# Hybrid attention layer, 16 heads in pairs: scores with q's high and low parts stacked in 128 rows

## What is computed

```python
h = rms_norm(x, norm_pre_g)
proj = einsum('bsd,de->bse', h, w_in)          # q, k, v, gate for 2 groups of 8 heads x 64, and 8 forget columns
# group A, per head:  logit[t,s] = q_t.k_s/8 + F[t] - F[s], causal, softmax, times v   (F: cumulated log forget gate)
# group B, per head:  logit[t,s] = q_t.k_s/8 - slope * (t - s), causal, softmax, times v
y = concat(y_a * silu(g_a), y_b * silu(g_b))
out = x + rms_norm(y @ w_out, norm_post_g)
```

## Time and profile before

| | before |
|---|---|
| median of 3 runs | 153.03 us |
| lowest, highest | 152.94, 153.65 us |
| profiled execution | 154.46 us |
| its span | 152.5 us |
| granted TensorE clock, mean | 0.977 of full speed |
| PE, DVE, ACT, POOL busy | 93%, 74%, 63%, 32% of the span |

### The profile page before, as it was taken

How to read it: one execution, slowest core, us unless ns; L and a number is a source line. 1 busy time by engine, 2 the same in 40 slices (tenths; PEclk the granted TensorE clock), 3 DMA queues, 4 the chain that set the end, 5 groups by cost and what they waited for, 6 DMA issues and landing times.

```text
span 152.5 us, 2938 instructions
## 1 busy us (share of the span) xinstructions
PE 142.0 (93%) x1020; PEld 133.6 (88%) x1020; DVE 112.8 (74%) x241; ACT 96.8 (63%) x199; POOL 48.1 (32%) x67
## 2 busy tenths in 40 slices
PE   7993999999999999999899999999999999999940
PEld 7992899999999989998899999999999888898840
DVE  0644918799999898856979897998979797220493
ACT  5455786717991799489487778686776855215430
POOL 7500000000000000708329393919375574201230
PEclk9999599999999999999999999999999999999995
DMA  3889995497789779880846463636451180000034
GB/s 106 233 255 390 392 373 181 148 349 254 241 258 315 260 299 413 314 267 9 221 156 192 140 198 132 210 140 209 138 171 35 49 295 0 0 4 0 0 116 160
DMA packets 14524, 29.05 MB, mean 191 GB/s; under 512 B 2472, under 2 KB 7088, under 8 KB 14128
## 3 DMA queue, kind: packets, MB, share of 16 engines
q1 hardware_dynamic: 14064, 27.57, 53.7%
q10 hardware_dynamic: 448, 1.32, 2.2%
HBM read 25.73 MB, written 1.06 MB: 176 GB/s over the span
## 4 chain that ended last, share of the span: by engine, by line
PE 64%; DVE 20%; DMA 5%; ACT 4%; SPq 3%; issue 1%; DVEq 0%; ACTq 0%
PE bank L801 26%; PE bank L960 15%; DVE w_lo L549 9%; PE bank L811 9%; PE bank L913 6%; DMA raw<-in_w_f 5%; ACT w_hi L369 3%; DVE wo_lo L630 2%; DVE h L594 2%; PE bank L894 2%; PE bank L896 2%; PE bank L895 2%; SPq L202 2%; DVE gate L638 2%; DVE v L607 1%
## 5 line engine op out<-in xcount | busy, mean ns | idle before, releaser
L549 DVE TENSOR_TENSOR w_lo<-raw,w_hi 128x1024 fp32r<-128x1024 f32 (+1 forms) x34 | 47.1, 1386 | 8.0 <-ACT w_hi L369 7.6
L369 ACT ACTIVATE w_hi<-raw 128x1024 fp32r<-128x1024 f32 (+1 forms) x34 | 35.8, 1059 | 6.2 <-DVE logits L645 3.6
L801 PE MATMUL bank<-h_hi,w_hi 128*128 128x256 f32 x128 | 35.8, 280 | 0.4 <-DVE h_lo L650 0.4
L801 PE MATMUL bank<-h_lo,w_hi 128*128 128x256 f32 x128 | 35.7, 279 | 0.0
L801 PE MATMUL bank<-h_hi,w_lo 128*128 128x256 f32 x128 | 35.7, 279 | 0.0
L306 POOL TENSOR_TENSOR bias<-squares,causal 128x256 f32<-128x256 f32 (+1 forms) x8 | 12.0, 1525 | 55.0 <-DMA squares<-decay_rows_scratch 55.0
L801 PEld LDWEIGHTS bank<-h_hi,w_hi 128*128 128x128 f32 x128 | 24.1, 188 | 1.1 <-DVE h_lo L650 0.6
L801 PEld LDWEIGHTS bank<-h_lo,w_hi 128*128 128x128 f32 x128 | 24.0, 188 | 0.5
L801 PEld LDWEIGHTS bank<-h_hi,w_lo 128*128 128x128 f32 x128 | 24.0, 188 | 0.0
L323 POOL TENSOR_TENSOR probs<-probs,row_inv 128x256 f32<-128x256 f32 (+1 forms) x16 | 12.9, 828 | 29.4 <-DVE row_inv L681 29.4
L464 ACT ACTIVATE probs<-logits,neg_max 128x128 f32<-128x128 f32 (+1 forms) x32 | 14.2, 445 | 7.8 <-DVE neg_max L675 7.8
(11 more groups left out here) (118 smaller groups left out, 308.7 us busy)
## 6 DMA issues: line engine op xcount, KB each, us to landing
raw<-in_w_units SPq DMA_DIRECT2D x30, 512.0 KB, 4.1
raw_out<-in_w_out SPq DMA_DIRECT2D x4, 512.0 KB, 4.6
v_pair<-v SPq DMA_DIRECT2D x8, 256.0 KB, 3.9
raw<-in_w_out SPq DMA_DIRECT2D x4, 512.0 KB, 3.4
h<-in_x SPq DMA_DIRECT2D x1, 1024.0 KB, 9.0
squares<-decay_rows_scratch ACTq DMA_DIRECT2D x1, 1024.0 KB, 8.0
x_t<-in_x SPq DMA_DIRECT2D x1, 1024.0 KB, 5.0
raw<-in_w_units SPq DMA_DIRECT2D x3, 256.0 KB, 4.3
```

The lines of the kernel that those rows point to most:

```text
L369: nc.scalar.activation(w[0][:, s, 0:width], raw[:, s, 0:width], ACT.Copy).then_inc(s_hi, 1)
L549: nc.vector.tensor_tensor(w[1][:, s, 0:width], raw[:, s, 0:width], w[0][:, s, 0:width].bitcast(F32), ALU.subtract).then_inc(s_lo, 1)
L801: last = nc.tensor.matmul(dst, stationary(a, j), moving(b, j), start=n == 1, stop=n == count * len(PASSES))
```

## The change

- q_hi becomes q_both (128 x 2 buffers x 2 heads x 256). For head a, ACT writes the high part in the head's own 64 rows (two instructions of 64 rows instead of one of 128). The other 64 rows get the head's q_lo by DMA.
- q_lo is made by two DVE instructions of 64 rows.
- k_wide_hi becomes k_twice: own rows k high from ACT, the other 64 rows the same k high, copied by DMA in place of zeros. k_lo keeps its zeros.
- The scores: per head, q_both x k_twice (high x high and low x high in one product over 128 rows) and q_both x k_lo (high x low). Eight matmuls of one head's 128 or 256 columns in place of six of 256 or 512.
- SP issues four copies per pair, 64 rows of 1 KB each: q_across(i), two, after q_lo(i); k_across(i), two, after k_hi(i). For pair 0 they stand ahead of SP's loop, for pair i in the loop's turn i: q_across between the two loads, k_across behind them.
- PE's scores wait for both pairs of copies and for k_lo.
- probs is the same buffer as logits; the row of ones moves to y32; one memset of POOL goes.

```diff
-        q_hi = sb("q_hi", [P, 2, SEQ], F32R)
+        q_both = sb("q_both", [P, 2, 2, SEQ], F32R)
-        k_wide = [sb(f"k_wide_{n}", [P, 2, SEQ], F32R) for n in PARTS]
+        k_twice, k_lo = sb("k_twice", [P, 2, SEQ], F32R), sb("k_lo", [P, 2, SEQ], F32R)
-        probs = sb("probs", [P, 2, NB])
+        probs = logits
...
+            def q_across(i):
+                sp.wait_ge(s_qlo, i + 1)
+                for a in range(2):
+                    sp.dma_start(q_both[head_rows[1 - a], i % 2, a, :].bitcast(F32),
+                                 q_lo[head_rows[a], i % 2, :].bitcast(F32)).then_inc(s_q_across[i % 2], 16)
+
+            def k_across(i):
+                sp.wait_ge(s_khi, 2 * i + 2)
+                for a in range(2):
+                    sp.dma_start(k_twice[head_rows[1 - a], a, :].bitcast(F32),
+                                 k_twice[head_rows[a], a, :].bitcast(F32)).then_inc(s_k_across[i % 2], 16)
+
+            q_across(0)
+            k_across(0)
             for i in range(1, PAIRS + 1):
...
-                for u in range(QK_0 + 6 + 2 * i, QK_0 + 8 + 2 * i):
+                for n, u in enumerate(range(QK_0 + 6 + 2 * i, QK_0 + 8 + 2 * i)):
+                    if i < PAIRS and n == 1:
+                        q_across(i)
                     if u < UNITS:
                         load_unit(u // RING, u % RING)
...
+                if i < PAIRS:
+                    k_across(i)
...
             def query_high(i, b):
...
-                nc.scalar.activation(q_hi[:, b, :], bank[0][:, 0:SEQ], ACT.Copy).then_inc(s_qhi, 1)
+                for a, own in enumerate(head_rows):
+                    nc.scalar.activation(q_both[own, b, a, :], bank[0][own, 0:SEQ], ACT.Copy).then_inc(s_qhi, 1)
...
             def query_low(i, b):
-                dve.wait_ge(s_qhi, i + 1)
-                nc.vector.tensor_tensor(q_lo[:, b, :], bank[0][:, 0:SEQ], q_hi[:, b, :].bitcast(F32),
-                                        ALU.subtract).then_inc(s_qlo, 1)
+                dve.wait_ge(s_qhi, 2 * i + 2)
+                for a, own in enumerate(head_rows):
+                    ins = nc.vector.tensor_tensor(q_lo[own, b, :], bank[0][own, 0:SEQ], q_both[own, b, a, :].bitcast(F32),
+                                                  ALU.subtract)
+                ins.then_inc(s_qlo, 1)
...
-            def scores(i, b):
-                pe.wait_ge(s_qhi, i + 1)
-                pe.wait_ge(s_qlo, i + 1)
-                pe.wait_ge(s_khi, 2 * i + 2)
+            def scores(i, b, loads):
+                pe.wait_ge(s_q_across[b], 32 * loads)
+                pe.wait_ge(s_k_across[b], 32 * loads)
                 pe.wait_ge(s_klo, 2 * i + 2)
                 for dst, rows, keys in ((s0_ps, slice(0, P), P), (s1_ps, slice(P, SEQ), SEQ)):
-                    nc.tensor.matmul(dst, q_hi[:, b, rows], k_wide[0][:, :, 0:keys], start=True, stop=False)
-                    nc.tensor.matmul(dst, q_hi[:, b, rows], k_wide[1][:, :, 0:keys], start=False, stop=False)
-                    last = nc.tensor.matmul(dst, q_lo[:, b, rows], k_wide[0][:, :, 0:keys], start=False, stop=True)
+                    for a in range(2):
+                        nc.tensor.matmul(dst[:, a, :], q_both[:, b, a, rows], k_twice[:, a, 0:keys],
+                                         start=a == 0, stop=False)
+                        last = nc.tensor.matmul(dst[:, a, :], q_both[:, b, a, rows], k_lo[:, a, 0:keys],
+                                                start=False, stop=a == 1)
                 last.then_inc(s_qk, 1)
```

More of the change, by code:

```diff
@@ L53 @@
 WARM_UP = 12
-N_CONST = 4
+N_CONST = 3
 PASSES = ((0, 0), (0, 1), (1, 0))
@@ L119, in hybrid_layer @@
         decay_row = logits[0:HEADS, 0, 0:SEQ]
-        ones_row = probs[0:HEADS, 0, 0:SEQ]
+        probs = logits
+        ones_row = y32[0:HEADS, :]
         junk = squares[:, :, :].rearrange("p a b -> p (a b)").rearrange("p (t d) -> p t d", t=TT)
@@ L171, in hybrid_layer @@
         s_khi, s_klo = sem("k_hi"), sem("k_lo")
+        s_q_across = [sem(f"q_lo_across{b}") for b in range(2)]
+        s_k_across = [sem(f"k_hi_across{b}") for b in range(2)]
         s_qk = sem("scores_ready")
@@ L282, in _ @@
                                base=0, pattern=[[-1, P]], channel_multiplier=1).then_inc(s_const, 1)
-            for part in k_wide:
-                pool.memset(part[:, :, :].bitcast(F32), 0.0).then_inc(s_const, 1)
+            pool.memset(k_lo[:, :, :].bitcast(F32), 0.0).then_inc(s_const, 1)
             pool.memset(ones_row, 1.0).then_inc(s_const, 1)
@@ L479, in key_high @@
                 for a, own in enumerate(head_rows):
-                    nc.scalar.activation(k_wide[0][own, a, :], bank[1][own, 0:SEQ], ACT.Copy).then_inc(s_khi, 1)
+                    nc.scalar.activation(k_twice[own, a, :], bank[1][own, 0:SEQ], ACT.Copy).then_inc(s_khi, 1)
             def gates_silu():
@@ L690, in key_low @@
                 for a, own in enumerate(head_rows):
-                    nc.vector.tensor_tensor(k_wide[1][own, a, :], bank[1][own, 0:SEQ],
-                                            k_wide[0][own, a, :].bitcast(F32), ALU.subtract).then_inc(s_klo, 1)
+                    nc.vector.tensor_tensor(k_lo[own, a, :], bank[1][own, 0:SEQ],
+                                            k_twice[own, a, :].bitcast(F32), ALU.subtract).then_inc(s_klo, 1)
             def gated(i):
@@ L931, in _ @@
             query(1, 1)
-            scores(0, 0)
+            scores(0, 0, 1)
             key(1, 1)
@@ L941, in attend @@
                 pe.wait_ge(s_logits, 4 * i - 4)
-                scores(i - 1, 1 - b)
+                scores(i - 1, 1 - b, loads + b)
                 key(i, b)
@@ L970, in _ @@
             pe.wait_ge(s_logits, 4 * PAIRS - 4)
-            scores(PAIRS - 1, 1)
+            scores(PAIRS - 1, 1, PAIRS // 2)
             out_part(1, range(0, 2))
```

## The result

The changed kernel takes 166.1 us in the median (165.59 to 167.66) against 152.99 for the kernel before on the same chip: a ratio of 1.084, with an interval of 1.0794 to 1.0885, or 13 us more. It is slower, as forecast, but by more than twice the 6 us and outside the range (162.5).

The account below looks back on a forecast made before the run. PE was taken as the bound, with a period of 8.33 us per pair and DVE's loop as long in the second half. Delay at scores(1) 5.6 plus 0.4 over pairs 2 to 7 gave +6.0: 159.0 us, range 156.0 to 162.5.

Parts of the forecast that it names:

- PE's new products: Scores on PE: 128-column matmuls taken at 0.11 us, 256-column ones at 0.12; a group 0.91 us, 0.15 less than now.
- the rival of plain f32 speed: Scores on PE: 128-column products cost 0.23 us each, group 1.39 us, total 160.8 us; chance 0.27.
- my 1.2: Scores on PE over eight pairs: 1.2 us saved by columns alone, if nothing waits.
- Pair 0, copies: Before scores(0): PE waits 2.6 us for the second key copy, issued at 64.6 and landed at 67.6.
- Pair 1: Before scores(1): key copy held behind SP's load waiting for unit_low, lands at 78.55; scores 5.6 us later, the main term.
- The clock: Rival: PE's clock falls behind the waits before scores(0) and scores(1), 0 to 1.6 us more, 160.6; chance 0.12.
- DVE's split: Two q_lo instructions of 64 rows: +0.43 us per pair on DVE, its loop 8.82 us, setting pairs 5 to 7.
- pairs 2 to 7: Six periods at 0.15 less give back 0.9 us, waits cost about 1.3: net +0.4 us.
- The faster rival: Copies land before their scores everywhere, 151.8 us; tested by pair 1's copy landing before k_lo(1) is done; chance 0.04.

Follow-up runs that it names:

- experiment 4: Changed kernel without the copies (their rows zeros) and without DVE's two q_lo instructions: ratio 0.9896 to the kernel before, -1.6 us.
- experiment 2: Changed kernel with the key's copy of pair 1 issued ahead of SP's load that waits for unit_low: ratio 1.0525 to the kernel before, +8.0 us.
- experiment 1: Changed kernel with idle PE products ahead of scores(0) and around transposes(0) to fill the waits: ratio 1.0653 to the kernel before, +10.0 us.
- experiment 8: Kernel of experiment 2 with 24 idle products ahead of scores(0): ratio 1.0529 to the kernel before, +8.1 us.
- experiment 7: Changed kernel without the copies, with four same-size transfers at their places into a buffer nobody reads: ratio 1.0147 to the kernel before, +2.2 us.
- experiment 5: Kernel before with only q_hi and q_lo each split into two instructions of 64 rows: ratio 1.0209 to the kernel before, +3.2 us.

## Why the prediction was wrong, point by point

**PE's new products: right.** The 128-column matmuls stand 0.11 us apart:

```profile
127.36 0.27 PE L918 MATMUL bank<-k_lo,q_both 128*128 128x128 f32 x1
127.47 0.27 PE L916 MATMUL bank<-k_twice,q_both 128*128 128x128 f32 x1
127.58 0.28 PE L918 MATMUL bank<-k_lo,q_both 128*128 128x128 f32 x1
```

Those with 256 columns stand 0.12 apart (128.03 to 128.38 in the chain above). So the rival of plain f32 speed (0.23) is out. The 81 ns that the Trainium skill (TensorE: Matmul & The Clock Gate, Back-to-back issue gap) gives is not reached here: the measured 0.11 decides. The group at 127.20, behind a wait, takes 1.18 us to 128.38, against 1.29 for the one at 72.94. Without hindrance the change gives 1.6 us (0.6 to 2.6, experiment 4), against my 1.2, though not all of that is PE's.

**Pair 0, copies: right, 1.0 us too small.** Scores(0) were to start 2.6 us late and started at 67.15, 2.3 later in the trace (64.83 before, in PE's timeline) and 3.6 counted from query(0). By the trace the copy of q_lo released it, which landed in 3.4 us; I had named the key's. Waits, place and order were as forecast.

**Pair 1: right mechanism, term mis-sized.** The delay was to grow by 3.0 us and grew by 5.2. Three items make it: the second copy lands in 3.5 us where I took 2.6; an issue takes 0.55 where I took 0.35, twice; and scores(0) ran at the lower clock (2.07 us from 67.15 to their end at 69.22 instead of 1.1). That SP's load ahead of the copy makes the wait long is shown by experiment 2.

**The clock: the step that failed.** I gave it 0.12 and at most 1.6 us, arguing that the work behind the waits has slack. It has none: the scores and the key product behind the second wait are the path, and they took 0.75 and 2.0 us more than at the full clock. The second fall cost 2.9 us (experiment 1), on top of 1 us within pair 1. I also took three microseconds at 0.50 from the earlier trace rows, and here the lower clock lasted over 6 us, twice. Without these 3.9 us the kernel would have taken some 162 us (my estimate, 166.1 less the two terms), just inside the range.

The trace before had the evidence that a fall was to be expected. The idle stretches of PE in all ten traces of this case bear it out, and show where it stops: behind each of the six of 2.3 us and more (2.34, 2.41, 2.64, 3.18, 3.21, 3.24) the granted clock went to the lower level. Of those between 1.6 and 2.1 us it did so behind three (1.64 in experiment 8, 2.04 in experiment 1, 2.08 in experiment 7) and not behind four (1.68, 1.77, 2.00, 2.08). Behind the shorter ones it never did. So a wait of 2.6 or 4 us should have carried the fall in the forecast and not in a rival.

**DVE's split: under-priced, and the engine that makes PE wait misnamed.** I took 0.43 us per pair from the durations of 64-row instructions. The right number is from start to start, 0.89 - 0.34 = 0.55, and DVE's period became 8.95, not 8.82. I also let it bite only in pairs 5 to 7 and only through the copies. Alone it costs 3.2 us (experiment 5, with ACT's split): 0.7 at scores(1), where q_lo stands ahead of k_lo, and the rest through row_inv, POOL and the transposes. In the changed kernel part of this lies within the copies' waits: DVE has time while PE waits.

**Sum.** 8.8 us by scores(1) where I had 5.6 (1.0 more in pair 0 and 2.2 more in pair 1), 2.7 from there to scores(2), the clock, where I had 0, and 2.1 over pairs 2 to 7 where I had 0.4: 13.6 against 6.0. The faster rival was excluded where I had put its test: the copy landed at 80.2, long after k_lo(1) at 76.5.

What stays open: how much the first fall of the clock costs by itself (experiments 1 and 8 both moved the wait), why both falls lasted twice as long in the changed kernel's trace as in the others, and why the group of 64-row products slows the product behind it by 0.2 us. Nor was pair 0's copy tried ahead of SP's load; it holds 3.6 of the 8.0 us that experiment 2 leaves.

## What to carry to other kernels

A new wait on a saturated engine is priced as wait plus what the engine's clock does afterwards: look for the idle stretches in your traces that were followed by the lower clock, take every new wait as long as those that always were as one that triggers it, and give the shorter ones a chance and not a certainty. A DMA that releases the bound engine must not stand behind another engine's wait or behind a large load in its queue; moving one copy forward gave back 4.8 of 13 us, some 1 us of it by a shorter fall of the clock. And before splitting an instruction over partition halves, read its cost from start to start, on an engine whose loop is as long as the bound engine's period.

## What the runs showed that I had not expected

- A transfer of 64 KB within SBUF landed in 1.9 to 2.0 us with nothing ahead of it, and in 3.4 to 3.5 us right behind a load of 512 KB; SP needs 0.55 us to issue one.
- Matmuls of 64 rows, one head's on rows 0 to 63 and the other's on rows 64 to 127, into different banks, ran side by side (12 in 0.89 us), and the key product after them took 3.02 us instead of 2.83.
- One DVE and one ACT instruction more per pair, with PE 93% busy, DVE at 74% and ACT at 63%, made the kernel 2.1% slower.
- The lower clock lasted over 6 us behind waits of 3.18 and 3.21 us in one trace, and about 3.5 us behind one of 3.24 us in another.
